# Four gated feed-forward stages of a ten-stage kernel: gate and up columns in one chunk, computed by features

## What is computed

```python
def swiglu(x, w_gu, w_down):                     # 1024 -> 2*2816 -> 1024
    g, u = jnp.split(x @ w_gu, 2, axis=-1)
    return (jax.nn.silu(g) * u) @ w_down
for l in range(2):                               # first block
    x = layer_norm(ALPHA * x + 0.5 * swiglu(x, ...), ...)      # ffn1
    x = layer_norm(ALPHA * x + (mixer_ab if l % 2 == 0 else mixer_c)(x), ...)
    x = layer_norm(ALPHA * x + 0.5 * swiglu(x, ...), ...)      # ffn1
for l in range(2):                               # second block
    x = x + mixer_g(rms_norm(x))
    x = x + jnp.square(relu(rms_norm(x) @ w_up)) @ w_down      # ffn2
```

## Time and profile before

| | |
|---|---|
| runs | 1905.2 us median (1904.73 to 1907.15) |
| the profiled execution | 1904.79 us, span 1903.0 us, mean granted clock 0.997 |
| PE matmul busy | 1873.5 us, 98% of the span |
| DVE, ACT busy | 1291.4 us (68%), 972.5 us (51%) |
| DMA, mean share of its engines | 55.3% for the queue of the weights |

### The profile page before, as it was taken

The page is one execution under the profiler, slowest core; times in us unless marked ns, Lnnn a source line. Parts: engine busy times, 40 slices in busy tenths (PEclk is TensorE's granted clock), DMA queues, the critical chain, the costliest instruction groups (busy, mean ns, idle before and its releaser), DMA issues.

```text
span 1903.0 us, 25523 instructions
## 1 busy us (share of the span) xinstructions
PE 1873.5 (98%) x9697; PEld 1592.3 (84%) x9697; DVE 1291.4 (68%) x1670; ACT 972.5 (51%) x1266; POOL 36.0 (2%) x67
## 2 busy tenths in 40 slices
PE   9999989999999999999989999999999999999998
PEld 7888877888888888788879888888888988888887
DVE  4565877465646678845576997687656798777754
ACT  5454564454445456545446446455544644555543
POOL 1010100000000000000000000000000000000000
PEclk9999999999999999999999999999999999999999
DMA  9666536665666665576545554466565554455662
GB/s 319 192 197 217 193 110 191 189 183 182 209 191 184 181 186 145 164 216 184 185 146 183 183 181 129 139 197 187 190 192 185 183 173 162 131 172 182 188 196 81
DMA packets 173578, 342.47 MB, mean 180 GB/s; under 512 B 10976, under 2 KB 11152, under 8 KB 173344
## 3 DMA queue, kind: packets, MB, share of 16 engines
q1 hardware_dynamic: 169360, 327.26, 55.3%
q0 software_dynamic: 4112, 13.77, 2.2%
HBM read 338.36 MB, written 1.05 MB: 178 GB/s over the span
## 4 chain that ended last, share of the span: by engine, by line
PE 82%; DVE 14%; ACT 2%; issue 1%; DMA 0%; SPq 0%; DVEq 0%; ACTq 0%
PE stream L2264 18%; PE stream L2266 17%; PE stream L2265 17%; PE stream L2451 6%; DVE wlo L1285 4%; PE stream L2452 3%; PE aux L2311 3%; PE stream L2431 2%; PE stream L2433 2%; PE stream L2432 2%; PE stream L2302 1%; PE stream L2293 1%; PE stream L2294 1%; PE stream L2370 1%; PE stream L2371 1%
## 5 line engine op out<-in xcount | busy, mean ns | idle before, releaser
L1285 DVE TENSOR_TENSOR wlo<-raw,whi 128x1024 fp32r<-128x1024 f32 x584 | 706.4, 1223 | 480.3 <-ACT whi L744 477.6
L744 ACT ACTIVATE whi<-raw 128x1024 fp32r<-128x1024 f32 x584 | 609.3, 1057 | 534.9 <-PE stream L2266 426.1
L2264 PE MATMUL stream<-whi,x_split 128*128 128x512 f32 x944 | 372.7, 395 | 2.7 <-DVE wlo L1285 2.7
L2266 PE MATMUL stream<-whi,x_split 128*128 128x512 f32 x944 | 368.1, 390 | 0.0
L2265 PE MATMUL stream<-wlo,x_split 128*128 128x512 f32 x944 | 367.5, 389 | 0.0
L2264 PE MATMUL stream<-whi,hhi 128*128 128x512 f32 x672 | 263.3, 392 | 0.0
L2266 PE MATMUL stream<-whi,hlo 128*128 128x512 f32 x672 | 261.6, 389 | 0.0
L2265 PE MATMUL stream<-wlo,hhi 128*128 128x512 f32 x672 | 261.5, 389 | 0.0
L2451 PE MATMUL stream<-x_split,whi 128*128 128x512 f32 x672 | 241.0, 398 | 0.0
L2264 PEld LDWEIGHTS stream<-whi,x_split 128*128 128x128 f32 x944 | 177.3, 188 | 38.4 <-issue 3.3
L2266 PEld LDWEIGHTS stream<-whi,x_split 128*128 128x128 f32 x944 | 177.2, 188 | 37.7
(11 more groups left out here) (345 smaller groups left out, 2091.0 us busy)
## 6 DMA issues: line engine op xcount, KB each, us to landing
raw<-ffn_w_gu SPq DMA_DIRECT2D x176, 512.0 KB, 4.3
raw<-w_in SPq DMA_DIRECT2D x136, 512.0 KB, 4.6
raw<-ffn_w_down SPq DMA_DIRECT2D x88, 512.0 KB, 3.8
raw<-w_up SPq DMA_DIRECT2D x64, 512.0 KB, 4.3
raw<-w_down SPq DMA_DIRECT2D x64, 512.0 KB, 4.4
raw<-c_w_in SPq DMA_DIRECT2D x24, 512.0 KB, 3.8
raw<-ab_w_in SPq DMA_DIRECT2D x20, 512.0 KB, 5.2
raw<-w_out SPq DMA_DIRECT2D x16, 512.0 KB, 3.7
```

The costliest lines, as they stand in the source:

```text
L744: act.activation(split_slots(lin, at, j)[0], raw[:, b % RAW], ACT.Copy).then_inc(hi_ready, 1)
L1285: dve.tensor_tensor(lo, raw[:, b % RAW], hi.bitcast(F32), ALU.subtract).then_inc(lo_ready, 1)
L2264: pe.matmul(bank[tt][:], hi, wh, start=kt == 0, stop=False)
L2266: mm = pe.matmul(bank[tt][:], lo, wh, start=False, stop=kt == last)
```

## The change

1. A chunk of a gated `up` now holds 256 gate columns and the 256 up columns that belong to them (`sides=2`). Its block is loaded by two DMAs of 256 KB, with pieces of 1 KB per row instead of 2 KB.
2. Chunk 0 stays `rows`, chunks 1 to 10 are `paired`. ACT evicts chunk 0 by quarters (Silu, Copy, Silu, Copy, 256 columns each), DVE multiplies, PE transposes 4 tiles behind chunk 1, and these alone.
3. In chunks 1 to 10, once the halves are added, ACT takes Silu of the two gate tiles in place (`gate`), DVE multiplies them with the two up tiles (`product`), ACT copies the result into `hhi` (`h_hi`), DVE subtracts into `hlo` (`h_lo`). Of the next splits, blocks 2 and 3 are made in the same turn as these, blocks 0 and 1 of the chunk after them.
4. A Silu over one column stands on ACT ahead of the eviction of chunk 0, behind the splits of chunk 1.
5. `down` waits for its tiles by block. The transposed parameters of the first stage come ahead of chunk 10.

```diff
-            up = Linear(io["ffn_w_gu"][l, i], D, 2 * D_FF)
+            up = Linear(io["ffn_w_gu"][l, i], D, 2 * D_FF, paired=range(1, 11), sides=2)
...
+    def transfers(self, slot, at, j):
...
+        n, rows = CH // self.sides, slice(j * BK * P, (j + 1) * BK * P)
+        return [(slot[:, :, i * n:(i + 1) * n],
+                 self.w[rows, bass.ds(at.c * n + i * self.w.shape[1] // self.sides, n)]
+                 .rearrange("(k p) n -> p k n", p=P)) for i in range(self.sides)]
...
# SyncE
-                    sp.dma_start(raw[:, slot], src.rearrange("(k p) n -> p k n", p=P)).then_inc(raw_in[slot], 16)
+                    for to, src in lin.transfers(raw[:, slot], at, j):
+                        sp.dma_start(to, src).then_inc(raw_in[slot], 16)
...
# ScalarE, ffn1
+                def gate(at):
+                    act.wait_ge(evicted, 2 * up.chunk(at) + 2)
+                    tiles = part_tiles(at)(0, 2)
+                    act.activation(tiles, tiles, ACT.Silu).then_inc(gate_made, 1)
+                def h_hi(at):
+                    act.wait_ge(h_made, h0 + at.c + 1)
+                    act.activation(hhi[:, bass.ds(2 * at.c, 2), :], part_tiles(at)(0, 2), ACT.Copy).then_inc(gated_hi, 1)
+                def body(at, to=up):
+                    before = At(at.like - 1, at.turn)
+                    split(up, at, 2, 3)
+                    gate(before)
+                    split(up, at, 3, 4)
+                    h_hi(before)
+                    split(to, At(at.like + 1, at.turn) if to is up else At(0), 0, 2)
+                    if at.like > 2:
+                        act.wait_ge(gated_lo, l0 + at.c - 2)
+                    copy_halves(up, at, part_tiles(at))
+                split(up, At(1))
+                act.wait_ge(eps_set, 1)
+                act.activation(small[:, 62:63], eps_cols[:, 0:1], ACT.Silu)
+                act.wait_ge(block_used, up.done(At(0)))
                 for tt in range(TT):
-                    bank = stream[up.banks(At(5)) + tt]
-                    act.activation(silu_gate[:, tt, 5 * CH:FF1], bank[:, 0:CH // 2], ACT.Silu)
-                    act.activation(up_part[1][:, tt, CH // 2:CH], bank[:, CH // 2:CH], ACT.Copy).then_inc(evicted, 1)
+                    bank = stream[up.banks(At(0)) + tt]
+                    act.activation(h_part[0][:, tt, 0:S], bank[:, 0:S], ACT.Silu)
+                    act.activation(h_part[0][:, tt, S:CH], bank[:, S:CH], ACT.Copy).then_inc(evicted, 1)
+                split(up, At(2), 0, 2)
+                copy_halves(up, At(1), part_tiles(At(1)))
+                turn_hi(by_tokens(hhi), 4)
...
# VectorE, ffn1
+                def body(at, to=up):
+                    before = At(at.like - 1, at.turn)
+                    rest(up, at, 2, 3)
+                    product(before)
+                    rest(up, at, 3, 4)
+                    h_lo(before)
+                    rest(to, At(at.like + 1, at.turn) if to is up else At(0), 0, 2)
+                    add_halves(up, at, part_tiles(at))
...
# TensorE, ffn1
-                chunks(pe, 1, 7, lambda at: rows(up, at, xhi, xlo), peel=1)
...
-                for c in range(6, up.n):
-                    if c > 6:
-                        rows(up, At(c), xhi, xlo)
...
-                    h_turn(c - 1, h0)
+                paired(up, At(1))
...
+                pe.wait_ge(h_made, h0 + 1)
+                bank = aux_bank()
+                for a in range(2):
+                    for tt in range(TT):
+                        t = pe.transpose(bank[:, (2 * a + tt) * P:(2 * a + tt + 1) * P],
+                                         h_part[0][:, tt, a * P:(a + 1) * P], ident)
+                t.then_inc(aux_full, 1)
+                chunks(pe, 2, up.n - 1, lambda at: paired(up, at))
...
+                paired(up, At(up.n - 1))
+                last_layer(st, hhi, hlo, ready=lambda j, tt: (gated_lo, l0 + j) if j else (aux_free, a0 + 1))
```

More of the change, by code:

```diff
@@ L254, with __init__ @@
 class Linear:
-    def __init__(self, w, k, n, order=(), walk=None, paired=()):
-        self.order, self.walk, self.paired = order, walk, paired
+    def __init__(self, w, k, n, order=(), walk=None, paired=(), sides=1):
+        self.order, self.walk, self.paired, self.sides = order, walk, paired, sides
         self.w, self.kb, self.n = w, k // (P * BK), n // CH
@@ L553, in program, with landed @@
                 place[lin.block(at, j)[0]] = first + n
+        transfers_of = [lin.sides for lin in lins for _ in range(lin.n * lin.kb)]
+        def landed(b):
+            return 16 * sum(transfers_of[b % RAW:b + 1:RAW])
         def split_count(b, turn=0):
@@ L888, in ffn1 @@
                 up, down = st.lins
-                split(up, At(0), SPLIT)
+                h0, l0 = seen.h, gated_before(st)
+                a0 = seen.aux
                 def gate(at):
[L892 to L897, removed]
-                for tt in range(TT):
-                    bank = stream[up.banks(At(5)) + tt]
-                    act.activation(silu_gate[:, tt, 5 * CH:FF1], bank[:, 0:CH // 2], ACT.Silu)
-                    act.activation(up_part[1][:, tt, CH // 2:CH], bank[:, CH // 2:CH], ACT.Copy).then_inc(evicted, 1)
@@ L902, in ffn1 @@
-                h0 = seen.h
-                for c in range(6, up.n):
[L904 to L907, removed]
-                    if c > 6:
[L910 to L914, removed]
+                    act.wait_ge(evicted, 2 * up.chunk(at) + 2)
@@ L915, in ffn1 @@
+                copy_halves(up, At(1), part_tiles(At(1)))
+                turn_hi(by_tokens(hhi), 4)
+                act.wait_ge(aux_full, a0 + 1)
+                body(At(2))
+                chunks(act, 3, up.n - 1, body)
+                if st is stages[0]:
+                    seen.aux += 1
+                body(At(up.n - 1), down)
+                split(down, At(0), 2, 3)
+                gate(At(up.n - 1))
+                split(down, At(0), 3, 4)
+                h_hi(At(up.n - 1))
                 split(down, At(0), SPLIT, SPLIT + 2)
-                h_turn_hi(*FF1_TILES[up.n - 1])
@@ L1217, in h_hi @@
                     act.activation(hhi[:, bass.ds(4 * at.c, 4), :],
-                                   relu_part[at.like % 2][:].rearrange("p a (b t) -> p (a b) t", b=2), ACT.Copy)\
+                                   h_part[at.like % 2][:].rearrange("p a (b t) -> p (a b) t", b=2), ACT.Copy)\
                         .then_inc(h_hi_ready, 1)
@@ L1222, in ffn2 @@
                 split(up, At(1))
[L1223 removed]
+                evict(up, At(0), lambda i: h_part[0][:, i, :], ACT.Relu)
                 split(up, At(2), 0, 2)
@@ L1524, in ffn1 @@
                 up, down = st.lins
[L1525 to L1547, removed]
+                l0 = gated_before(st)
+                def product(at):
+                    dve.wait_ge(gate_made, l0 + at.c)
+                    part = part_tiles(at)
+                    dve.tensor_tensor(part(0, 2), part(0, 2), part(2, 4), ALU.mult).then_inc(h_made, 1)
@@ new lines, in ffn1 @@
+                rest(up, At(1))
+                dve.wait_ge(evicted, 2 * up.c0 + 2)
+                part = h_part[0][:]
+                dve.tensor_tensor(part[:, :, 0:S], part[:, :, 0:S], part[:, :, S:CH], ALU.mult).then_inc(h_made, 1)
+                rest(up, At(2), 0, 2)
+                add_halves(up, At(1), part_tiles(At(1)))
+                turn_lo(by_tokens(hhi), by_tokens(hlo), 4)
+                chunks(dve, 2, up.n - 1, body)
+                if st is stages[0]:
+                    copy_params()
+                    dve.wait_ge(const_in, 32)
@@ L1548, in ffn1 @@
+                body(At(up.n - 1), down)
+                rest(down, At(0), 2, 3)
+                product(At(up.n - 1))
+                rest(down, At(0), 3, 4)
+                h_lo(At(up.n - 1))
                 rest(down, At(0), SPLIT, SPLIT + 2)
-                h_turn_lo(*FF1_TILES[up.n - 1])
                 last_layer(st, SPLIT + 2)
@@ L2163, in square @@
                     dve.wait_ge(evicted, 2 * up.chunk(at) + 2)
-                    part = relu_part[at.like % 2][:]
+                    part = h_part[at.like % 2][:]
                     dve.scalar_tensor_tensor(part, part, 0.0, part, ALU.max, ALU.mult).then_inc(h_made, 1)
@@ L2514, in ffn1 @@
                     rows(up, At(0), xhi, xlo, ready=x_ready())
[L2515 to L2526 removed]
+                paired(up, At(1))
+                h0, a0, l0 = seen.h, seen.aux, gated_before(st)
+                pe.wait_ge(h_made, h0 + 1)
[6 more added lines that the diff above has]
+                chunks(pe, 2, up.n - 1, lambda at: paired(up, at))
+                if st is stages[0]:
+                    turn_params()
+                paired(up, At(up.n - 1))
+                last_layer(st, hhi, hlo, ready=lambda j, tt: (gated_lo, l0 + j) if j else (aux_free, a0 + 1))
+                seen.h = h0 + up.n
             def turn_params():
```

53 lines of the change are left out of this document (23 added, 30 removed).

## The result

The changed kernel takes 1913.2 us (median of 6 runs, 1911.91 to 1916.13) against 1905.4 of the kernel before, measured beside it: ratio 1.0039, 95% interval 1.003 to 1.0049. It is slower by 7.4 us by the ratio and 7.8 by the medians; the forecast was +3.5 us, and the measured time lies outside the range of 1904.6 to 1912.2. The profiled execution took 1911.97 us, its span is 1910.4 us, 7.4 us more than the earlier trace rows show.

A forecast was written before the change was run, and what follows sets the result against it. PE's own stream was taken to bound the gated stages. Stages 2 to 4 gave 3 x (1.68 - 0.76) = +2.8 us, stage 1 +0.4, the start +0.3: +3.5, 1908.7 us on the median; range 1904.6 to 1912.2, own bounds 1907 to 1910.

The forecast's parts named there:

- Part 2: PE's stream in a gated stage, new form: 11.25 us per paired chunk, 172.2 us against 172.97, 0.76 us less.
- Part 3: New PE wait at output tile 2 for chunk 0's eviction: 1.68 us in gated stages 2 to 4, 1.18 in the first.
- the sum: Gated stages 2 to 4 +2.8 us, stage 1 +0.4, start +0.3: total +3.5 us.
- Part 4: ACT, DVE and DMA work in gated up stays hidden, DMA 0 to 15% dearer; the program's start costs 0.3 us.
- A: Rival, 8%: the wait at output tile 2 doesn't appear; sum -2.7 us, 1902.5 us.
- B: Rival, 7%: ACT's order pushes the last copies late by 0.3 us in each of 36 chunks; +11, 1919 us.
- D: Rival, 3%: weight loads of paired chunks hide, a chunk takes 10.88 us; 14.8 us less than forecast, 1894.
- E: Rival, 2%: 1 KB pieces make DMA the bound, some 40% longer up, over 150 us more.
- F: Rival, 2%: ACT pauses once more behind each table load by about 1.28 us; 5.1 us in all, 1914.
- C: Rival, 6%: the new wait near a gated stage's start brings one more clock fall, about 3 us; 1912.
- The list of what to see: Signs expected in the changed profile, among them first weight matmul at 9.4 to 9.8 in place of 9.34.

The follow-up runs named there:

- a_silu_first: The changed kernel with the one-column Silu ahead of the splits of chunk 1 instead of behind them: 1907.22 us, ratio 1.0011 to the kernel before.
- a_order: The changed kernel with the one-column Silu first and chunk 0's eviction ahead of the split of block 3 of chunk 1: 1904.97 us, ratio 0.9994.
- a_no_silu: The changed kernel without the one-column Silu: 1911.0 us, ratio 1.0031 to the kernel before.
- a_filler: The changed kernel with 7 instead of 2 filler products on PE ahead of the first weight matmul: 1913.28 us, ratio 1.0046.
- after_again: The changed kernel, unaltered, measured once more: 1912.26 us, ratio 1.0034 to the kernel before.
- b_two_cols: The kernel before with each block of a gated up loaded by two DMAs by column halves (1 KB pieces): 1906.83 us, ratio 1.001.
- b_two_rows: The kernel before with each block of a gated up loaded by two DMAs by row halves (2 KB pieces): 1906.58 us, ratio 1.0006.
- b_const: The kernel before with the loads of constants and masks put off until chunk 2 is done: 1905.99 us, ratio 0.9993.
- a_order_const: a_order with the loads of constants and masks put off until chunk 2 is done: 1904.79 us, ratio 0.999 to the kernel before.
- a_order_const_fill: a_order_const with 7 instead of 2 filler products on PE at the start: 1903.97 us, ratio 0.9987 to the kernel before.

## Why the prediction was wrong

**The stream and the wait were right.** Part 2 gave 11.25 us per paired chunk, measured 11.28; 0.35 for the transposes, measured 0.36; 59.17 for `down`, measured 59.17. Part 3 gave 11.33 + 1.68 = 13.01 for chunk 1 in stages 2 to 4, measured 13.05, 12.97 and 12.97. `a_silu_first` takes the load off the path and gets 5.3 to 5.9 us back, where Part 3 had 6.2 for all four waits, and `a_order` removes the wait in every stage: its mechanism is shown to the instruction. For the first stage Part 3 had 12.51, measured 12.55, but this agreement is luck: only in this profile had the half clock held chunk 0 back until block 7 was there. In the others chunk 1 of the first stage takes 13.31 (`a_no_silu`), 13.96 (`a_filler`) and 15.33 us (`after_again`, with 3.4 us at half clock in it). The one-column Silu was put at 0.15 us, and is 0.11. The stages together are 0.8 us dearer than the sum had them, which the paired chunk's 0.03 us (36 times, 1.1 us) covers.

**The step that failed is the start**, in Part 4: "I take 0.3, as the data of x and block 0 fill the queue before the second issue matters", with bounds of 0 to 0.95, and the claim on DMA just ahead of it, "it stays hidden". Three things were in it.
1. The second issue does matter. Chunk 0 ends 0.7 us later at full clock (22.30 and 22.31 in `after_again` and `a_no_silu`, against 21.62), 0.9 in `b_two_cols`. That lies within the bounds, but at their upper end.
2. I read DMA's share only in the steady stretch, where it is in fact no higher after (0.65 in `up`, 0.71 before; the forecast had 0.7 to 0.8). In the first 30 us the engines are full. A block in 1 KB pieces takes 11% longer there, which is inside the 0 to 15% that Part 4 allowed; what Part 4 didn't have are the loads of the constants, which come beside block 7. It lands at 23.47 in `a_no_silu` and 23.79 in `after_again`, and is split at 23.50 and 23.82 in place of some 22.6 (PE frees its slot 0.3 us behind chunk 0's end): +0.9 to +1.3. The cover that Part 4 claimed for DMA is gone at this one place, because the paired form has made the eviction behind block 7's split a thing that PE waits for. Parts 3 and 4 were each right elsewhere, and their meeting was missed: `b_two_cols` has the late block and loses nothing to it, `a_order` has it and loses nothing, the changed kernel does.
3. The clock. In the profiled execution PE waited 2.8 us for the first weight block, until 10.20, and the clock was at half from 9.54 to 16.37. That made chunk 0 end at 24.97 and not 22.30, 2.7 us. It also hid thing 2, so that at the end of chunk 1 1.9 us were left of it (37.52 against 35.62 in `a_no_silu`). The length of the wait alone doesn't decide it: at the same place `b_two_cols` and `a_order` waited 3.0 and 3.1 us and stayed at full clock, `b_two_rows` and `a_silu_first` waited 2.2 and 2.3 us and fell. What decides is open.

**The sum, put right.** The kernel's own cost is 3.9 (stages) + 0.7 + 0.9 to 1.3 = 5.5 to 5.9 us. A second way gives much the same. Half of the time at half clock is the most that it can have cost; taken off the span, the profiles read as below. The last column does the same for all executions of each kernel (5 to 33), of which span and mean granted clock are on record: it is the mean of span times clock, for the kernel before in each of the three groups. The mean counts the last 1.3 to 3.9 us of a span too, which are at half clock in every profile and which the third column leaves out; so it lies 0.6 to 2 us lower than the fourth column would.

| kernel | span | time at half clock | span less half of it | mean of span x clock |
|---|---|---|---|---|
| before | 1903.0 | 6.8 | 1899.6 | 1898.0, 1897.9, 1897.8 |
| b_two_cols, b_two_rows | 1906.3, 1905.0 | 13.7, 10.2 | 1899.5, 1899.9 | 1898.6, 1898.9 |
| b_const | 1905.4 | 13.7 | 1898.6 | 1898.4 |
| after, after_again | 1910.4, 1915.6 | 10.2, 20.5 | 1905.3, 1905.4 | 1904.0, 1903.8 |
| a_no_silu, a_filler | 1908.6, 1910.6 | 6.8, 10.2 | 1905.2, 1905.5 | 1904.4, 1905.1 |
| a_silu_first | 1903.4 | 6.8 | 1900.0 | 1898.7 |
| a_order, a_order_const, a_order_const_fill | 1906.1, 1904.9, 1901.9 | 17.1, 13.7, 6.8 | 1897.6, 1898.1, 1898.5 | 1897.6, 1897.8, 1896.5 |

A single profile is good to about 1 us, since a stretch with waits in it loses less than half; the means are good to some 0.3 to 0.4 us (single executions scatter by about 1), `a_filler`'s and `a_no_silu`'s to 0.7 to 0.9. By them the changed kernel's own cost is 6.0 to 6.1 us, and the two kernels with two DMAs stand 0.6 and 0.9 us above the one before, as their late chunk 0 has it. The medians differ by 7.3 to 7.8 us; the rest is time at half clock, of which the changed kernel had 1 to 2 us more per execution by the same means (it lost at most 8.0 and 7.3 us to it, the kernel before 5.8, 6.9 and 5.9). Whether the change brings these on stays open: `a_no_silu`, with the same start, lost at most 5.1.

**The rivals.** A (no wait), B (ACT's order), D (weight loads hide), E (DMA-bound) and F (a drain) are out: the wait is there, chunks take 11.28 us, the share in `up` is 0.65, and the one-column Silu starts 0.02 us behind the load's end. C, one more fall of the clock for about 3 us, came true in part: in the first profile a fall cost 2.7 us at chunk 0, but it stood at the start of the program, where I didn't expect it, and over all executions the clock accounts for only 1 to 2 us of the difference. The list of what to see said 9.4 to 9.8 for the first weight matmul; 10.20, and 9.86 and 9.89 in the later profiles, was the sign of the failed step.

## What to carry to other kernels

A chunk form that uses all PSUM banks puts the eviction before it on the path, and with it all that stands ahead of the eviction in its engine's order: move table loads into idle time and late splits behind it, before the form is judged (here the ratio to the kernel before went from 1.0039 to 0.9994 by order alone). Read the start of a kernel as a stage of its own, with its own DMA share and issues per block: the steady stretch said 0.65, the first 30 us over 1, with loads in them that the steady stretch doesn't have. Where two parts of a forecast are each hidden by the same engine's slack, ask what happens when both come at once.

## What the hardware showed beside

Where it was the only edit, a second DMA issue per block made the splits of blocks 0 and 1 0.6 to 0.9 us later, although both DMAs together move the same bytes. With full engines 1 KB pieces moved 361 to 366 GB/s, 2 KB pieces 384 to 405, and a block of 512 KB took 1.51 against 1.36 us; with the engines at 0.65 to 0.71 there was nothing to see of it. Loads of 1.4 and 0.45 MB on another queue made a block issued 1.4 us before them land 4.8 us later (24.10 against 19.27). The granted clock fell to half in different places in two executions of one kernel (9.5 and 989 us in one, 29, 278, 742, 995 and 1005 in the other), up to 5 and 10 us lost for the same instructions: a single profile can't price a change of some us here, unless the stretches at half clock are taken out first. Span times mean granted clock, averaged over all executions, gave 1898.0, 1897.9 and 1897.8 us for the kernel before in three groups whose medians differed by 1.5 us.
